# Prompt probabilities transposed in one burst per head pair, selection and prompt values behind the keys, and a later place in the DMA queue for part of the last values

## The chip, the cores and the metric

The kernel runs on one core of a Trainium2 chip. The metric is the device time of one execution in microseconds, taken as the median of several runs. Engines are named as in the profile: PE is TensorE (PEld its weight loads), DVE is VectorE, ACT is ScalarE, POOL is GpSimd, SP is SyncE (SPq its issues of transfers). TensorE has two clock levels, 1.2 and 2.4 GHz; the profile gives the granted clock as a share of the higher one.

## What is computed

One inference step of a two-layer decoder trunk with a width of 2048, for one prompt of 256 tokens and eight decode sequences of eight tokens each, with 2048 past positions in a cache. Each layer is

```python
h = rms_norm(x, g_mix); p = h @ w_in              # columns split among A, B, C
A: dilated sliding-window attention, 8 heads of 64: branches (128,1), (512,4), (2048,16)
B: RWKV-7 time mixing, 8 heads of 64
C: sliding-window attention, window 128, 16 query heads on 2 key heads, with sinks
x = x + concat(A, B, C) @ w_out
x = x + SwiGLU(rms_norm(x, g_ffn))
```

For the prompt, attention is over its own 256 tokens; for a decode token it is over the cached keys and values and the new tokens of its sequence:

```python
s = einsum('bthd,btjhd->bthj', q, k_gathered) * ATTN_SCALE
p = exp(s - logsumexp(s))
o = einsum('bthj,btjhd->bthd', p, v_gathered)
```

The outputs are the new hidden states, the new keys and values, and the new states of B. All data are float32.

## The kernel before

Each engine has its own hand-written instruction stream, and the engines meet at named semaphores: `take("x")` waits for the next count of `x`, `.then_inc` raises it. Nothing reorders the streams, so the order of the lines of an engine is the order in which it works, and an instruction that waits holds back all that stands behind it on its engine. SP issues nearly all transfers, also in the order of its lines.

A layer first streams the projection `w_in` (with B's preparation beside it), then runs B's recurrence, then **attention**, then the projection `w_out` and the SwiGLU weights. The change touches attention alone. The streams of matrix products are bound by TensorE and take most of the time.

Attention has two kinds of work, woven into one another:

- **Prompt work** is twelve pairs of heads, `p` = 0 to 11 (four of A, eight of C). For a pair, TensorE makes the scores (`prompt_scores`, into PSUM banks 0 and 1). VectorE scales, masks and finds the maxima (`front`). ScalarE takes the exponentials (`exp`), VectorE the reciprocal of the sums (`back`), ScalarE multiplies by it (`scale`). TensorE transposes the probabilities, three blocks of 128x128 for each of the two heads, into bank 2; ScalarE copies them to `ppt` (`turned_probs` on both engines). TensorE multiplies them with the values into bank 3 (`prompt_values`), and ScalarE copies the result out (`output`).
- **Sample work** is four passes `q` = 0 to 3, each for two decode sequences. SP loads the cached keys of the two sequences (`cK`, ten tiles of 128x512 each, in three groups per sequence, issued by `next_keys`) and the cached values (`cV`, `next_values`). VectorE transposes the keys in place in 32x32 blocks (`turn`, six groups per pass). TensorE multiplies them with the queries into banks 4 to 7 (`keys`: eight blocks of 32 small matmuls, then the new tokens and the C heads). VectorE scales, masks and finds maxima (`scores`), ScalarE takes exponentials (`exps`), TensorE transposes the probabilities (`probabilities`), ScalarE copies them (`turned_sample`), TensorE multiplies them with the values (`values`). VectorE normalises into `om` (`weighted`); TensorE picks each head's own rows by a matmul with a constant (`select`, into bank 3), and VectorE copies these into `pT` (`outputs`). `window_keys` and `query_rows` prepare the next pass.

In each pass the prompt work of up to three pairs, called `a`, `b` and `carry`, stands between the steps of the sample work. In pass `q` before the change `carry` is pair 3q+2, `a` is 3q+3, `b` is 3q+4 and `c`, whose scores only are made here, is 3q+5; the last pass has `carry` alone. Before the change, the selection of the previous pass, the scores of `a`, the two halves of the transposes of `carry` and the prompt values of `carry` all stand between the eight blocks of `keys`; the transposes and values of `a` and the scores of `b` follow `keys`; those of `b` follow `values`.

For the last pass the values need a place of their own: the early half (sequence 7, `cX`) lies where the outgoing states `Sout` were, so SP waits until these are written (`souts`). Before the change it does so in pass index 1, behind the second keys and ahead of the values of that pass. The other half goes where the first key tile was, once the keys of the last pass are used.

The matmul helper has two lines only: L1492 is every `mm`, L1493 every `tr` (transpose by a matmul with the identity). So in the rows a step is told by its tiles: `PS<-cK,qd` is `keys`, `PS<-con,psm` the transposes of prompt probabilities, `PS<-ppt,tk` the prompt values, `PS<-con,om` the selection, `PS<-con,smA` the sample probabilities, `PS<-cV,ptA` the sample values, `PS<-hh,wh` the output projection behind attention.

Of the kernel before, what the change touches and what calls it, by code (L numbers as in the profile page):

```python
# [37 lines left out]
P = 128  # L38
D = 2048
DEPTH = 2  # L40
SEQ = 256
# [5 lines left out]
HD = 64  # L47
# [127 lines left out]
def build(nc, I, O, at):  # L175
    ctx = ExitStack()
    with ctx:
# [99 lines left out]
        ppt = place("ppt", [P, 2, 384], RW + 44032)  # L277
# [48 lines left out]
        def partners(q):  # L326

            return (3 * q + 3, 3 * q + 4, 3 * q + 5) if q < LASTQ else (None, None, None)
# [34 lines left out]
        def _(sp):  # L363
# [75 lines left out]
            for l in range(DEPTH):  # L439
# [183 lines left out]
        def _(act):  # L623
# [155 lines left out]
            for l in range(DEPTH):  # L779
# [102 lines left out]
                def turned_probs(p):  # L882
                    for h in range(2):
                        take("PT")
                        if p and not h:
                            act.wait_ge(sem["O"], PAIRS * l + p)
                        act.activation(ppt[:, h], PS[:, 2, 0:384], ACT.Copy).then_inc(sem["ptc"], 1)  # L887

                def output(p):
                    take("O")  # L890
                    act.activation(pT[:, tile_of(p), PROMPT], PS[:, 3, 0:SEQ], ACT.Copy).then_inc(sem["oc"], 1)
# [28 lines left out]
                scale(0)  # L920
                turned_probs(0)
                exp(1)
                output(0)
                scale(1)
# [3 lines left out]
                for q in range(NB // 2):  # L928
                    a, b, c = partners(q)
                    carry = 3 * q + 2  # L930
                    exp(carry)
                    scale(carry)
                    turned_probs(carry)
                    if q < LASTQ:
                        exp(a)
                    output(carry)
                    if q < LASTQ:
                        scale(a)
                        turned_probs(a)
                        output(a)  # L940
                    if q == 0:
                        act.wait_ge(sem["snk"], 64 * (l + 1))
                    exps(q)
                    turned_sample(q)
                    if q < LASTQ:
                        query_rows(q + 1)
                        exp(b)
                        scale(b)
                        turned_probs(b)
                        output(b)  # L950
# [5 lines left out]
                split(n0, 0, 0, kts, nd)  # L956
                for g, t0 in enumerate((QA, BR, QC, QC + 4)):
# [20 lines left out]
        def _(dve):  # L978
# [349 lines left out]
            def attention(l):  # L1328
                def front(p):
# [3 lines left out]
                    if p >= 2:  # L1333
                        dve.wait_ge(sem["PT"], 2 * (PAIRS * l + p - 1))
# [50 lines left out]
                def outputs(q):  # L1385
                    take("sel")
                    o = SEQ + 2 * TS * q
                    for hf in range(2):
                        dve.tensor_copy(pT[:, QA + 2 * hf:QA + 2 * hf + 2, o:o + 2 * TS],
                                        PS[:, 3, 256:320].rearrange("p (f h t) -> p h f t", f=2, h=2)[:, hf])  # L1390
                    for b2 in range(2):
                        a = dve.tensor_copy(pT[:, QC:QC + 8, o + b2 * TS:o + b2 * TS + TS],
                                            PS[:, 3, 320 + 64 * b2:384 + 64 * b2].rearrange("p (i t) -> p i t", i=8))
# [5 lines left out]
                turn(0, 1, 2)  # L1399
                back(1)  # L1400
                turn(0, 2, 4)
                front(2)
                turn(0, 4, 6)
                for q in range(NB // 2):
                    a, b, c = partners(q)
                    if q:
                        outputs(q - 1)
                    back(3 * q + 2)
                    if q < LASTQ:
                        front(a)  # L1410
                        back(a)
# [9 lines left out]
                    if q < LASTQ:  # L1421
                        front(c)
# [62 lines left out]
        def _(pe):  # L1485
# [366 lines left out]
            def attention(l):  # L1852
# [30 lines left out]
                def turned_probs(p, h):  # L1883

                    take("pn", 1 - h)
                    if p or h:
                        pe.wait_ge(sem["ptc"], 2 * (PAIRS * l + p) + h)
                    for i in range(3):
# [215 lines left out]
```

## Time and profile before

| | before |
|---|---|
| median of 3 runs | 3384.05 us (3379.69 to 3388.35) |
| the profiled execution | 3381.76 us |
| its span, first to last instruction | 3380.0 us |
| TensorE busy | 3198.1 us, 95% of the span |
| VectorE busy | 1757.8 us, 52% |
| ScalarE busy | 1150.6 us, 34% |
| bytes moved by DMA | 501.29 MB, 148 GB/s over the span |
| granted TensorE clock, mean | 0.962 |

The page of the profile gives busy times over the whole span. The attention stage of the first layer lies at 467 to 648 us, that of the second at 2131 to 2314 us. In the views, a bracket behind a row, such as [7.52 <-DMA cK], is how long the engine stood idle before that instruction and what released it; "issue" means that it waited for nothing that the profile shows. A matmul count is in hardware passes, two for each of these float32 instructions where the row shows the doubled number. The rows of SPq are issues of transfers, not the transfers themselves.

### The profile page before, as it was taken

To read this page: it belongs to the slowest core of one execution; us is meant where nothing else is said; L and a number is where in the kernel's file an instruction comes from. 1 tells how busy PE (TensorE), PEld (TensorE's weight loads), DVE (VectorE), ACT (ScalarE), POOL (GpSimd) and SP (SyncE) were. 2 spreads that over 40 slices of the span, in tenths; PEclk is the share of its full clock that TensorE was granted. 3 is DMA by queue.
4 is the path that set the end of the run, shared out by engine and by line. 5 is a ranking of instruction groups with operands and counts; after the bars stand their busy time and mean duration, and the time that the engine had idled before them with its cause. 6 is when DMAs were issued, how large, how long until landed. Compare 5 with 4: busy or idle time off the path is not lost. (4 is left out here: it accounts for less than half of the span.)

```text
span 3380.0 us, 62858 instructions
## 1 busy us (share of the span) xinstructions
PE 3198.1 (95%) x26358; PEld 3021.7 (89%) x26358; DVE 1757.8 (52%) x2117; ACT 1150.6 (34%) x1543; POOL 74.3 (2%) x157
## 2 busy tenths in 40 slices
PE   8999877799999999999999988778999999999998
PEld 7999744699999999999999986447999999999998
DVE  5455555555555454454545665654555544545544
ACT  3332244433222322322434313543422223223234
POOL 1000010000000000000000000100000000000000
PEclk9999878899999999999999998788999999999999
DMA  6562047665554554654565610677655555545554
GB/s 199 164 135 65 2 155 294 195 151 151 150 149 137 159 149 137 165 149 137 150 187 137 137 27 2 225 286 176 149 149 149 149 140 159 149 139 160 137 148 131
DMA packets 848709, 501.29 MB, mean 148 GB/s; under 512 B 96608, under 2 KB 823152, under 8 KB 848112
## 3 DMA queue, kind: packets, MB, share of 16 engines
q1 hardware_dynamic: 848108, 499.01, 52.6%
q8 instruction: 115, 1.88, 0.2%
q14 instruction: 34, 0.28, 0.0%
q10 hardware_dynamic: 452, 0.11, 0.0%
HBM read 485.71 MB, written 13.37 MB: 148 GB/s over the span
## 5 line engine op out<-in xcount | busy, mean ns | idle before, releaser
L634 ACT ACTIVATE wh<-raw 128x2048 fp32r<-128x2048 f32 (+1 forms) x408 | 711.7, 1744 | 1236.3 <-PE PS L1492 1200.3
L994 DVE TENSOR_TENSOR wl<-raw,wh 128x2048 fp32r<-128x2048 f32 (+1 forms) x408 | 848.8, 2080 | 412.1 <-ACT wh L634 411.4
L1492 PE MATMUL PS<-fh,wh 128*128 128x320 f32 x2816 | 870.6, 309 | 0.0
L1492 PE MATMUL PS<-fl,wh 128*128 128x320 f32 x2816 | 870.1, 309 | 0.0
L1492 PE MATMUL PS<-fh,wl 128*128 128x320 f32 x2816 | 870.1, 309 | 0.0
L1492 PEld LDWEIGHTS PS<-fl,wh 128*128 128x128 f32 x2816 | 528.6, 188 | 0.2
L1492 PEld LDWEIGHTS PS<-fh,wh 128*128 128x128 f32 x2816 | 528.6, 188 | 0.2
L1492 PEld LDWEIGHTS PS<-fh,wl 128*128 128x128 f32 x2816 | 528.6, 188 | 0.0
L1492 PE MATMUL PS<-hh,wh 128*128 128x320 f32 (+2 forms) x1696 | 518.4, 311 | 5.6 <-DVE wl L994 5.6
L1492 PE MATMUL PS<-hh,wl 128*128 128x320 f32 (+2 forms) x1696 | 513.5, 309 | 0.0
L1492 PE MATMUL PS<-hl,wh 128*128 128x320 f32 x1664 | 513.2, 312 | 0.0
L1492 PE MATMUL PS<-ah,wh 128*128 128x320 f32 x1408 | 435.7, 309 | 0.7 <-DVE wl L994 0.5
L1492 PE MATMUL PS<-al,wh 128*128 128x320 f32 x1408 | 435.1, 309 | 0.0
L1492 PE MATMUL PS<-ah,wl 128*128 128x320 f32 x1408 | 435.1, 309 | 0.0
L1492 PEld LDWEIGHTS PS<-hh,wh 128*128 128x128 f32 x1696 | 315.1, 188 | 9.4 <-DVE wl L994 6.1
L1492 PEld LDWEIGHTS PS<-hl,wh 128*128 128x128 f32 x1664 | 314.9, 190 | 1.6 <-DVE hl L1433 0.2
L1492 PEld LDWEIGHTS PS<-hh,wl 128*128 128x128 f32 x1696 | 315.2, 189 | 0.0
L1492 PEld LDWEIGHTS PS<-ah,wh 128*128 128x128 f32 x1408 | 264.3, 188 | 1.4 <-issue 1.2
L1492 PEld LDWEIGHTS PS<-al,wh 128*128 128x128 f32 x1408 | 264.3, 188 | 0.0
L1492 PEld LDWEIGHTS PS<-ah,wl 128*128 128x128 f32 x1408 | 264.3, 188 | 0.0
L663 ACT ACTIVATE ge<-gt 128x320 f32<-128x320 f32 x88 | 41.5, 472 | 488.2 <-DVE gt L1034 488.2
L1034 DVE TENSOR_TENSOR gt<-PS,rsb 128x320 f32<-128x320 f32 x88 | 43.3, 492 | 226.0 <-PE PS L1492 226.0
(327 smaller groups left out, 2554.9 us busy)
## 6 DMA issues: line engine op xcount, KB each, us to landing
raw<-in_w_gate SPq DMA_DIRECT2D x88, 1024.0 KB, 5.6
raw<-in_w_up SPq DMA_DIRECT2D x88, 1024.0 KB, 5.6
raw<-in_w_down SPq DMA_DIRECT2D x128, 704.0 KB, 4.8
raw<-in_w_in SPq DMA_DIRECT2D x56, 1024.0 KB, 5.6
cK<-in_cache_a_k SPq DMA_DIRECT2D x80, 512.0 KB, 9.0
cV<-in_cache_a_v SPq DMA_DIRECT2D x60, 512.0 KB, 10.6
raw<-in_w_in SPq DMA_DIRECT2D x32, 512.0 KB, 5.6
raw<-in_w_out SPq DMA_DIRECT2D x32, 512.0 KB, 4.8
```

What stands on the lines that cost most here:

```text
L634: act.activation(wh[j][:, 0:kts], raw[j][:, 0:kts], ACT.Copy).then_inc(sem["wh"], 1)
L663: act.activation(ge[:], gt[:], ACT.Tanh, scale=0.5).then_inc(sem["gexp"], 1)
L994: tt(wl[j][:, 0:kts], raw[j][:, 0:kts], wh[j][:, 0:kts].bitcast(F32), ALU.subtract).then_inc(sem["wl"], 1)
L1034: tt(gt[:], PS[:, 0, 0:TOK], rsb[:], ALU.mult).then_inc(sem["ev"], 1)
L1492: mm = lambda out, lhsT, rhs, start=True, stop=True: pe.matmul(out, lhsT, rhs, start=start, stop=stop, skip_group_check=True)
```

## The change

Three things are changed, all in attention.

1. The transposes of both heads of a pair are made in one go, six blocks into 768 columns that span bank 2 and the first half of bank 3, and ScalarE copies them with one instruction. The prompt values go into the second half of bank 3, so the transposes of a pair now wait until the previous pair's output has been copied.
2. The pairs are dealt out anew: passes 0 and 1 have `carry`, `a` and `b`, pass 2 has `carry` and `a`, pass 3 has `carry` and `a`. Within `keys` only the scores of `a` (behind the fourth block) and the transposes of `carry` (ahead of the last block) remain. Behind `keys` come the prompt values of `carry`, then transposes and values of `a`, the scores of `b`, and the selection of the previous pass, which now goes into bank 7 and waits for `scores` to have read it (`smb`). The transposes of `b` stand inside `values`, behind its eighth step. On VectorE `front(carry)` to `back(a)` stand ahead of `scores`, `outputs` behind it, and `back(b)` one key group earlier. ScalarE's order follows.
3. SP issues the early half of the last values in pass index 2, behind the third keys, and not in pass index 1. The wait for the written states moves with it.

The core of the diff:

```diff
         def partners(q):
-            return (3 * q + 3, 3 * q + 4, 3 * q + 5) if q < LASTQ else (None, None, None)
+            if q < 2:
+                return 3 * q + 2, 3 * q + 3, 3 * q + 4, 3 * q + 5
+            return (8, 9, None, 10) if q == 2 else (10, 11, None, None)
...
                     if q == 1:
                         states_out()
+                    if q == 2:
                         sp.wait_ge(sem["souts"], 16 * 18 * (l + 1))
                         for quad in range(3):
                             cache(NB - 1, "V", quad)
...
                 def turned_probs(p):
-                    for h in range(2):
-                        take("PT")
-                        if p and not h:
-                            act.wait_ge(sem["O"], PAIRS * l + p)
-                        act.activation(ppt[:, h], PS[:, 2, 0:384], ACT.Copy).then_inc(sem["ptc"], 1)
+                    take("PT")
+                    act.activation(ppt[:], PS[:, 2:4, :].rearrange("p b c -> p (b c)")[:, 0:768], ACT.Copy).then_inc(sem["ptc"], 1)
...
                 for q in range(NB // 2):
-                    a, b, c = partners(q)
-                    carry = 3 * q + 2
+                    carry, a, b, c = partners(q)
                     exp(carry)
                     scale(carry)
+                    exp(a)
                     turned_probs(carry)
-                    if q < LASTQ:
-                        exp(a)
+                    scale(a)
                     output(carry)
-                    if q < LASTQ:
-                        scale(a)
-                        turned_probs(a)
-                        output(a)
+                    turned_probs(a)
                     if q == 0:
                         act.wait_ge(sem["snk"], 64 * (l + 1))
                     exps(q)
+                    output(a)
                     turned_sample(q)
...
-                turn(0, 2, 4)
-                front(2)
-                turn(0, 4, 6)
+                turn(0, 3, 6)
                 for q in range(NB // 2):
-                    a, b, c = partners(q)
+                    carry, a, b, c = partners(q)
+                    front(carry)
+                    back(carry)
+                    front(a)
+                    back(a)
+                    scores(q)
                     if q:
                         outputs(q - 1)
-                    back(3 * q + 2)
                     if q < LASTQ:
-                        front(a)
-                        back(a)
-                    scores(q)
-                    if q < LASTQ:
-                        front(b)
-                        turn(q + 1, 0, 5)
-                        back(b)
-                        turn(q + 1, 5, 6)
+                        if b:
+                            front(b)
+                            turn(q + 1, 0, 4)
+                            back(b)
+                            turn(q + 1, 4, 6)
+                        else:
+                            turn(q + 1, 0, 6)
                     else:
                         split(start_of(l, "out"), 0, KT)
                     weighted(q)
-                    if q < LASTQ:
-                        front(c)
...
-                            if (h, jj) == (0, 0):
-                                if q:
-                                    select(q - 1)
-                                if q < LASTQ:
-                                    prompt_scores(a)
-                            elif (h, jj) == (1, 0):
-                                turned_probs(carry, 0)
-                            elif (h, jj) == (2, 0):
-                                turned_probs(carry, 1)
+                            if (h, jj) == (1, 1):
+                                prompt_scores(a)
                             elif (h, jj) == (3, 0):
-                                prompt_values(carry)
+                                turned_probs(carry)
...
-                        if k == 3 and q < LASTQ:
-                            prompt_scores(partners(q)[2])
+                        if q < LASTQ:
+                            carry, a, b, c = partners(q)
+                            if k == 3:
+                                prompt_scores(c)
+                            elif k == 7 and b:
+                                turned_probs(b)
...
                     keys(q)
-                    if q < LASTQ:
-                        for h in range(2):
-                            turned_probs(a, h)
-                        prompt_values(a)
+                    prompt_values(carry)
+                    turned_probs(a)
+                    prompt_values(a)
+                    if b:
                         prompt_scores(b)
+                    if q:
+                        pe.wait_ge(sem["smb"], 4 * l + q + 1)
+                        select(q - 1)
                     probabilities(q)
                     values(q)
```

## Rows read from the trace of the kernel before

**Rows 1.** Windows, the attention stages: length, busy us per engine, clock, DMA share, GB/s.

```profile
466.90:647.90 181.00, 129.86 (x1961) 77.16 (x1961) 98.51 (x149) 89.25 (x290) 5.73 (x27) 0.80 0.75 266
2130.90:2314.00 183.10, 129.00 (x1965) 76.72 (x1965) 98.28 (x149) 88.90 (x290) 5.25 (x28) 0.82 0.75 263
```

**Rows 2.** Timeline, first layer: start us, length us; first matmul of each pass, then projection.

```profile
490.91 1.38 PE L1492 MATMUL PS<-cK,qd 32*32 32x320 f32 x32 [2.21 <-DVE cK L1354]
...
528.20 0.83 PE L1492 MATMUL PS<-cK,qd 32*32 32x320 f32 x32 [0.47 <-ACT kcT L857]
...
575.24 1.38 PE L1492 MATMUL PS<-cK,qd 32*32 32x320 f32 x32 [0.47 <-ACT kcT L857]
...
614.02 0.83 PE L1492 MATMUL PS<-cK,qd 32*32 32x320 f32 x32 [0.47 <-ACT kcT L857]
...
648.31 2.16 PE L1492 MATMUL PS<-hh,wh 128*128 128x256 f32 x16
```

**Rows 3.** The same of the second layer.

```profile
2154.58 1.38 PE L1492 MATMUL PS<-cK,qd 32*32 32x320 f32 x32 [3.84 <-DVE cK L1354]
...
2191.75 1.38 PE L1492 MATMUL PS<-cK,qd 32*32 32x320 f32 x32 [0.47 <-ACT kcT L857]
...
2240.45 1.38 PE L1492 MATMUL PS<-cK,qd 32*32 32x320 f32 x32 [0.47 <-ACT kcT L857]
...
2279.60 0.83 PE L1492 MATMUL PS<-cK,qd 32*32 32x320 f32 x32 [0.47 <-ACT kcT L857]
...
2313.95 2.16 PE L1492 MATMUL PS<-hh,wh 128*128 128x256 f32 x16
```

**Rows 4.** Timeline, the legs of the first and second pass, first layer.

```profile
512.14 2.57 PE L1493 MATMUL PS<-con,smA 128*128 128x128 f32 x11 [3.38 <-ACT ssk L900]
...
532.72 0.31 PEld L1493 LDWEIGHTS PS<-con,psm 128*128 128x128 f32 x3 [0.74 <-ACT psm L879]
...
542.17 1.69 DVE L1364 SCALAR_TENSOR_TENSOR smA<-PS,con 128x320 f32<-128x320 f32 x4 [3.66 <-PE PS L1492]
...
546.59 1.42 ACT L897 ACTIVATE smA<-smA,snm 128x1344 f32<-128x1344 f32 x1 [1.11 <-DVE snm L1370]
...
549.22 2.13 PE L1493 MATMUL PS<-con,smA 128*128 128x128 f32 x11 [3.31 <-ACT ssk L900]
```

**Rows 5.** Timeline, steps that the change moves: transposes, prompt values, selection.

```profile
524.17 0.55 PE L1493 MATMUL PS<-con,psm 128*128 128x128 f32 x3
...
526.49 0.87 PE L1492 MATMUL PS<-ppt,tk 128*64 128x256 f32 x8 [0.58 <-ACT ppt L887]
...
528.96 0.63 PE L1492 MATMUL PS<-con,om 128*128 128x32 f32 x4
```

**Rows 6.** Timeline, the third keys: the issue ahead of them and the waits behind.

```profile
529.17 1.89 SPq L476 DMA_DIRECT2D cX<-in_cache_a_v  x3
...
556.12 2.31 DVE L1354 STREAM_TRANSPOSE cK<-cK 128x2048 f32<-128x2048 f32 x1 [7.52 <-DMA cK<-in_cache_a_k]
...
565.42 2.31 DVE L1354 STREAM_TRANSPOSE cK<-cK 128x2048 f32<-128x2048 f32 x1 [0.25 <-DMA cK<-in_cache_a_k]
...
569.57 0.90 PE L1493 MATMUL PS<-con,psm 128*128 128x128 f32 x3 [5.47 <-ACT psm L879]
```

**Rows 7.** Windows of 5 us, columns as in the first group.

```profile
555.00:560.00 5.00, 5.00 (x40) 3.18 (x40) 3.72 (x2) 1.98 (x10) 0.00 (x0) 0.50 1.03 402
580.00:585.00 5.00, 5.00 (x132) 2.38 (x131) 1.97 (x3) 1.60 (x5) 0.00 (x0) 0.61 0.01 3
```

**Rows 8.** DMA issues of the whole run: count, KB each, us to landing.

```profile
cK<-in_cache_a_k SPq DMA_DIRECT2D x80, 512.0 KB, 9.0
```

**Rows 9.** Groups by line, whole run: count, busy us, mean ns, idle before.

```profile
L887 ACT ACTIVATE ppt<-PS 128x384 f32<-128x384 f32 x48 | 23.5, 490 | 61.2 <-PE PS L1493 61.2
L907 ACT ACTIVATE ptA<-PS 128x512 f32<-128x512 f32 x16 | 9.5, 597 | 10.5 <-PE PS L1493 10.5
L1354 DVE STREAM_TRANSPOSE cK<-cK 128x2048 f32<-128x2048 f32 x32 | 72.9, 2294 | 21.2 <-DMA cK<-in_cache_a_k 21.0
```

More of the change, by code:

```diff
@@ L276, in build @@
         smC = place("smC", [P, 2, 192], RS + 26880)
-        ppt = place("ppt", [P, 2, 384], RW + 44032)
+        ppt = place("ppt", [P, 768], RW + 44032)
         nm = [place(f"nm{i}", [P, 2, 2], RS + 29184 + 64 * i) for i in range(2)]
@@ L920, in _ @@
                 scale(0)
+                exp(1)
                 turned_probs(0)
-                exp(1)
+                scale(1)
                 output(0)
-                scale(1)
                 turned_probs(1)
@@ L946, in _ @@
                         query_rows(q + 1)
[L947 to L950, printed above, removed]
+                        if b:
+                            exp(b)
+                            scale(b)
+                            turned_probs(b)
+                            output(b)
                         window_keys()
@@ L956, in _ @@
                 split(n0, 0, 0, kts, nd)
+                act.wait_ge(sem["oc"], PAIRS * (l + 1))
                 for g, t0 in enumerate((QA, BR, QC, QC + 4)):
@@ L1881, in prompt_scores, with turned_probs @@
                     a.then_inc(sem["S"], 1)
[L1883 to L1888, printed above, removed]
-                        a = tr(PS[:, 2, i * P:(i + 1) * P], psm[p % 2][:, h, i * P:(i + 1) * P])
+                def turned_probs(p):
+                    take("pn")
+                    if p:
+                        pe.wait_ge(sem["oc"], PAIRS * l + p)
+                    bank = PS[:, 2:4, :].rearrange("p b c -> p (b c)")
+                    for i in range(6):
+                        a = tr(bank[:, i * P:(i + 1) * P], psm[p % 2][:, i // 3, i % 3 * P:(i % 3 + 1) * P])
                     a.then_inc(sem["PT"], 1)
                 def prompt_values(p):
-                    pe.wait_ge(sem["ptc"], 2 * (PAIRS * l + p) + 2)
-                    if p:
-                        pe.wait_ge(sem["oc"], PAIRS * l + p)
-                    if p >= 5 and p % 3 == 2:
-                        pe.wait_ge(sem["bo"], 4 * l + p // 3)
+                    pe.wait_ge(sem["ptc"], PAIRS * l + p + 1)
                     for kt in range(2):
@@ L1902, in prompt_values @@
                             vals = tk[1 if p < 4 else 2][:, kt, c0:c0 + HD]
-                            out = PS[h * HD:h * HD + HD, 3, P * kt:SEQ]
-                            a = mm(out, vals, ppt[:, h, 0:SEQ] if kt == 0 else ppt[:, h, SEQ:384], kt == 0, kt == 1)
+                            out = PS[h * HD:h * HD + HD, 3, SEQ + P * kt:512]
+                            a = mm(out, vals, ppt[:, 384 * h:384 * h + SEQ] if kt == 0 else ppt[:, 384 * h + SEQ:384 * h + 384], kt == 0, kt == 1)
                     a.then_inc(sem["O"], 1)
                 def keys(q):
-                    a, b, c = partners(q)
-                    carry = 3 * q + 2
+                    carry, a, b, c = partners(q)
                     pe.wait_ge(sem["ktc"], 8 * l + 2 * q + 2)
@@ L2008, in attention @@
                 prompt_scores(1)
-                for h in range(2):
-                    turned_probs(0, h)
+                turned_probs(0)
                 prompt_values(0)
                 prompt_scores(2)
-                for h in range(2):
-                    turned_probs(1, h)
+                turned_probs(1)
                 prompt_values(1)
@@ L2017, in attention @@
                 for q in range(NB // 2):
-                    a, b, c = partners(q)
+                    carry, a, b, c = partners(q)
                     keys(q)
-                    if q < LASTQ:
-                        for h in range(2):
-                            turned_probs(a, h)
-                        prompt_values(a)
+                    prompt_values(carry)
+                    turned_probs(a)
+                    prompt_values(a)
+                    if b:
                         prompt_scores(b)
+                    if q:
+                        pe.wait_ge(sem["smb"], 4 * l + q + 1)
+                        select(q - 1)
                     probabilities(q)
@@ L2027, in attention @@
                     if q < LASTQ:
-                        for h in range(2):
-                            turned_probs(b, h)
-                        prompt_values(b)
+                        if b:
+                            prompt_values(b)
                         window_keys(q + 1)
```

18 lines of the change are left out of this document (10 added, 8 removed).

## The prediction

> **What bounds the kernel now.** I read the stretches by stage first. The change lies only in the two attention stages, and there TensorE is busy 129.9 of 181.0 us and 129.0 of 183.1 us, with the DMA engines at 0.75 of their time [rows 1]; everywhere else the kernel is left as it is. No engine is full in these stages, so the order of waits sets their length, and I read that order from the timeline. A stage is a short prologue and four passes, one per pair of decode sequences. In the first layer the key matmuls of the passes begin at 490.91, 528.20, 575.24 and 614.02, and the output projection at 648.31 [rows 2]: passes of 37.3, 47.0, 38.8 and 34.3 us. The second layer has 37.2, 48.7, 39.2 and 34.4 us [rows 3].
>
> A pass has four legs, one behind the other: the **key leg** (matmuls on the old keys, until VectorE can start the scores), the **gap** (mask and maxima on VectorE, exponentials on ScalarE), the **value leg** (transposes of the probabilities, then the matmuls on the old values) and the **tail** to the next key matmul. In the second pass the key leg is 528.20 to 542.17 = 14.0 us and the gap 542.17 to 549.22 = 7.05 us [rows 2, 4]. In the first pass the value leg is 512.14 to 524.17 = 12.0 us and the tail 524.17 to 528.20 = 4.0 us [rows 2, 4, 5].
>
> The second pass is ten microseconds longer than its neighbours, and the reason stands in one place: VectorE sat 7.52 us for the third keys, and TensorE later 5.47 us for the scaled prompt probabilities that VectorE reached only behind the transposes of those keys [rows 6]. The keys were late because SyncE had queued the early half of the last values, at 529.17, ahead of the values of pass 1 and of these keys [rows 6]. The DMA engines moved 402 GB/s at 555 to 560 us and 3 GB/s at 580 to 585 us [rows 7]: a queue in the wrong order, not a lack of bandwidth.
>
> **Part 1, the last values behind the third keys.** Ten issues of 512 KB make one pass's keys (80 issues over eight passes) [rows 8], so 5.4 MB with the small cache; values are the same and the early half of the last values is 2.6 MB. From 529.17 to 565.42, when the fifth of the six key groups had landed [rows 6], the queue moved 2.6 + 5.4 + 4.7 = 12.7 MB: 351 GB/s with the start. After the change only 10.1 MB stand there: 28.8 us. They also start earlier: pass 0 is about 3.5 us shorter up to there (below), and SyncE no longer waits at this point for the states it has written. I put the start at 525.5, so the fifth group lands at 554.3 in place of 565.4. What is moved costs later: the 2.6 MB go in front of the values of pass 2 and the fourth keys. At 402 GB/s the 13.3 MB of those three down to the fifth fourth-key group last 33 us, to 587.4. The values of pass 2 are needed about 582 and land about 575; the fourth keys come just in time (part 3).
>
> **Part 2, work leaves the path.** Selection (528.96 to the next step, 1.0 us) and the prompt values (0.87 us) leave the key leg, and the 0.74 us for which the first half of the transposes waited goes too, because the burst now stands one block from the end [rows 4, 5]. Key leg: 14.0 - 1.0 - 0.9 - 0.7 = 11.4 us. They go into the gap, in which TensorE has about 7 us and gets prompt values (0.9), six transposes, prompt values (0.9), prompt scores (0.9) and selection (1.0), some 5 us with the ScalarE copies between them. Costed at nothing, then; if that cover is gone, the gap grows by what sticks out. Behind the second pair's copy ScalarE has the sample exponentials. By my order that copy ends 3.3 us after the key leg (prompt values 0.9, their copy 0.4, transposes 0.9, copy 0.8, handovers) and the maxima come 4.4 us after it (542.17 to 546.59 [rows 4]), so about 1 us is in hand.
>
> The burst itself: two copies of 128x384 take 0.49 us each, a 128x512 copy 0.60 us [rows 9]. One of 768 is not in the trace: between 0.60 and 0.98; carried on along the two rows it is 0.82. Take 0.82. Now the value matmuls start 2.3 us after the first transpose (524.17 to 526.49) [rows 5]; six transposes, about 0.9 us by two of the 0.55 us rows [rows 5] less their overlap, then 0.82 and two handovers make about 2.0.
>
> In passes 0 and 1 the burst of pair b moves inside the value leg (+1.0 us), so that its copy runs beside the last two value steps. The tail shrinks from 4.0 to about 2.0: values 0.9, window keys, two copies. VectorE's weighting, which the next keys wait for as well, runs beside it and is the shorter. Pass 2 loses pair b altogether (its pair goes into the gap of pass 3), so 3 us of tail go and its value leg keeps its 12.0.
>
> **Part 3, what VectorE and the queues then do.** `outputs` moves behind `scores` and waits for selection, some 2 us later than the scores' maxima; behind it stand `front(b)` and the key transposes, 2.3 us for each of the four large ones [rows 9] and half of it for the two of half the size, 11.5 us together. In pass 1 these transposes start near 545.6 and the fourth ends near 553.8; pair b's scale follows and TensorE waits about 1.2 us for it. The sixth ends near 558, the values near 557.5, the weighting near 559: three ends within 1.5 us. Pass 2: the fourth keys' last transpose ends about 590.7, the weighting, behind the values, about 592. So after the change DMA, VectorE and TensorE are nearly level.
>
> **Sum.** Prologue: TensorE waits 2.21 and 3.84 us for the first keys' transposes [rows 2, 3]; `front(2)` moves behind them, so at most that much: I take 2.0 and 3.0. Pass 0: key leg 13.7 (it starts at the lower clock, its first block 1.38 in place of 0.83 us [rows 2]), gap 7.1, value leg 13.2, tail 2.0: 36.0, a gain of 1.3 and 1.2. Pass 1: 11.4 + 7.1 + 14.2 (with the 1.2 us wait) + 2.1 = 34.8: 12.2 and 13.9. Pass 2: 11.6 + 7.1 + 12.1 + 1.8 = 32.6: 6.2 and 6.6. Pass 3: prompt scores come into its key leg, selection and values go, with the wait about 1.8 each. In the first layer the passes would then begin at 488.9, 524.9, 559.7 and 592.3 and the projection at 624.8. First layer 23.5, second 26.5, together 50 us. Against the profiled execution of 3381.76 us (span 3380.0) that is 3331.8; the median of the three runs, 3384.05, lies 2.3 us higher: 3334.
>
> **Rivals.** *The queue stays the bound.* If the DMA engines hold 350 and not 402 GB/s over the now unbroken 62 us, the third keys end 3 us later and the fourth 8.5 us later than worked out, which nothing hides: 17 us given back, 3351. For it: the 351 GB/s above, and the saturated queue without the pause at 580 us. Against: 402 to 410 once it runs.
>
> *ScalarE late.* If the chain of the second pair is 2.5 us later than I have it, the exponentials start 1.5 us late in each of eight passes: 12 us, 3346. For it: only 1 us is in hand. Against: the chain stands ahead of the exponentials now as well.
>
> *The clock, upward.* The granted clock was 0.50 at 555 to 560 us, the 1.2 GHz level, behind an idle time of TensorE of 3.31 us before the probabilities [rows 4, 7]; the key block takes 1.38 us there and 0.83 us at the 2.4 GHz level [rows 2]. With the gap filled, the longest idle time inside a pass is about 2 us. If all of the passes then run at the higher level, pass 0's key leg gives 1.2 us and pass 3's values about 1.5: 5 us in two layers, 3329. The Trainium skill ("TensorE: Matmul & The Clock Gate", Part 1, "What's actually happening") says that the throttled state is the default and activity releases it, which speaks for this rival. The trace agrees [rows 4, 7]; by that rule alone the time would be 3329.
>
> *The clock, downward: slower than before.* The new idle times are shorter but more numerous. If they hold TensorE at the lower level through the passes, a key leg of eight blocks alone costs 8 x 0.55 = 4.4 us more, in proportion 7 for the whole leg, 4 for the value leg and 2 for the rest: 13 us a pass, 104 in all, 3438. From about half of that on the gain is gone. Against it: now the low level follows the long idle times, and these go.
>
> *It doesn't do what it says:* the gap work sticks out by as much as it saves and only the queue's order acts. Then passes 1 alone give, some 9 us each: 3366.
>
> **How the numbers follow.** Forecast 0.55, the queue 0.16, ScalarE 0.08, clock upward 0.10, only the queue's order 0.04, clock half downward (no change) 0.03, wholly downward 0.04. Range 3316 to 3356: it takes the forecast with its bounds (copy 0.60 to 0.98 us on twelve bursts a layer, prologue, a bubble of 1 us in each key leg), both middle rivals and the upward clock, and leaves 0.11 out above plus some tail below. About 0.3% (10 us) is what a measurement of this kernel can tell from no change. Faster 0.93, within it 0.03, slower 0.04.
>
> **What would show it.** Right: the second pass no longer than its neighbours, about 35 us; no VectorE wait of 7 us on keys; one 768-column copy per pair near 0.82 us; selection and prompt values between the key leg and the probabilities, with the gap still near 7.1 us; key legs near 11.4. Wrong, if VectorE waits for fourth keys, if the exponentials start more than 0.2 us behind the maxima, or if the granted clock of the stages falls below the 0.80 and 0.82 of now [rows 1].

## The result, and the profile after

| | before | after |
|---|---|---|
| median | 3381.87 us (3378.37 to 3388.35, 4 runs) | 3341.43 us (3331.34 to 3343.31, 4 runs) |
| ratio, 95% interval | | 0.9873 [0.9858, 0.9888] |
| profiled execution, its span | 3381.76, 3380.0 us | 3341.29, 3339.5 us |
| mean granted clock | 0.962 | 0.968 |

The change saves 40.5 us by the spans. 3334 was predicted, 7 us too low, inside the range of 3316 to 3356. Windows over the attention stages of the kernel after (columns as in [rows 1]):

```profile
465.40:627.40 162.00, 121.82 (x1964) 76.63 (x1965) 98.30 (x149) 86.29 (x278) 6.55 (x32) 0.84 0.84 298
2110.00:2272.60 162.60, 120.67 (x1964) 76.77 (x1965) 98.42 (x149) 86.40 (x278) 5.86 (x28) 0.86 0.84 296
```

Against [rows 1] the stages are 19.0 and 20.5 us shorter, all but one microsecond of the gain. Timeline of TensorE, first layer: the first key matmuls of the passes and the output projection, which answer to [rows 2].

```profile
487.08 1.38 PE L1490 MATMUL PS<-cK,qd 32*32 32x320 f32 x32 [0.47 <-ACT kcT L860]
...
520.46 0.83 PE L1490 MATMUL PS<-cK,qd 32*32 32x320 f32 x32 [0.47 <-ACT kcT L860]
...
560.83 1.59 PE L1490 MATMUL PS<-cK,qd 32*32 32x320 f32 x58 [0.47 <-ACT kcT L860]
...
595.30 0.96 PE L1490 MATMUL PS<-cK,qd 32*32 32x320 f32 x33 [0.92 <-DVE omC L1381]
...
627.42 2.16 PE L1490 MATMUL PS<-hh,wh 128*128 128x256 f32 x16
```

The second layer has its passes at 2129.45, 2161.65, 2202.63 and 2240.46 and the projection at 2272.61. Gains by pass, from these times and [rows 2, 3]:

| gain, us, first / second layer | predicted | measured | pass is now |
|---|---|---|---|
| prologue | 2.0 / 3.0 | 2.3 / 4.2 | 21.7 / 19.5 |
| pass 0 | 1.3 / 1.2 | 3.9 / 5.0 | 33.4 / 32.2 |
| pass 1 | 12.2 / 13.9 | 6.7 / 7.7 | 40.4 / 41.0 |
| pass 2 | 6.2 / 6.6 | 4.3 / 1.3 | 34.5 / 37.8 |
| pass 3 | 1.8 / 1.8 | 2.2 / 2.2 | 32.1 / 32.2 |
| stage | 23.5 / 26.5 | 19.4 / 20.4 | |

Three steps of the second pass came out close to the forecast or better. The start of the scores on VectorE, of the exponentials on ScalarE and of the transposes of the probabilities, which answer to [rows 4]:

```profile
530.45 1.68 DVE L1363 SCALAR_TENSOR_TENSOR smA<-PS,con 128x320 f32<-128x320 f32 x4 [0.92 <-PE PS L1490]
...
534.88 1.42 ACT L897 ACTIVATE smA<-smA,snm 128x1344 f32<-128x1344 f32 x1 [1.45 <-DVE snm L1369]
...
537.50 1.42 PE L1491 MATMUL PS<-con,smA 128*128 128x128 f32 x11 [1.26 <-ACT ssk L900]
```

Key leg 520.46 to 530.45 = 10.0 us, gap 7.05 us as before, and the exponentials still wait for the maxima, not for the copy of the burst. That copy, in the groups by line (count, busy us, mean ns, idle before):

```profile
L887 ACT ACTIVATE ppt<-PS 128x768 f32<-128x768 f32 x24 | 19.3, 803 | 19.2 <-PE PS L1491 19.2
```

0.80 us, where 0.82 was taken. What fell short stands in pass 1, at the third keys, as in [rows 6]:

```profile
544.39 2.31 DVE L1353 STREAM_TRANSPOSE cK<-cK 128x2048 f32<-128x2048 f32 x1 [5.45 <-DMA cK<-in_cache_a_k]
...
550.96 2.31 DVE L1353 STREAM_TRANSPOSE cK<-cK 128x2048 f32<-128x2048 f32 x1 [0.59 <-DMA cK<-in_cache_a_k]
...
553.60 3.44 DVE L1353 STREAM_TRANSPOSE cK<-cK 128x2048 f32<-128x2048 f32 x2
...
555.11 1.54 PE L1491 MATMUL PS<-con,psm 128*128 128x128 f32 x6 [7.73 <-ACT psm L882]
```

and in the value leg of pass 2:

```profile
579.16 1.54 PE L1491 MATMUL PS<-con,smA 128*128 128x128 f32 x11 [2.12 <-ACT ssk L900]
...
586.61 3.64 PE L1490 MATMUL PS<-cV,ptA 128*32 128x256 f32 x32
```

In pass 1 VectorE still waits 5.45 us for keys and TensorE 7.73 us, more than the 5.47 us of before, for pair b's scaled probabilities behind four transposes. In pass 2 the 32 value matmuls take 3.64 us, at the lower clock; in pass 0 they take 1.93.

### The profile page after: what moved, and what is told of

It reads as the page before. It is cut to its first block, busy times and chain, and to the rows that moved or that the text cites. A ratio compares the mean times of both kernels' runs of the same rounds, so it can differ in the third digit from the quotient of the medians.

```text
span 3339.5 us, 62764 instructions
## 1 busy us (share of the span) xinstructions
PE 3181.0 (95%) x26358; PEld 3019.1 (90%) x26358; DVE 1757.0 (53%) x2117; ACT 1145.1 (34%) x1519; POOL 73.8 (2%) x157
## 4 chain that ended last, share of the span: by engine, by line
PE 89%; DVE 4%; SPq 2%; DMA 2%; ACT 1%; issue 1%; ACTq 0%; DVEq 0%
PE PS L1490 87%; PE PS L1491 2%; DMA cK<-in_cache_a_k 1%; SPq L510 1%; SPq L478 1%; DVE wl L993 0%; DMA raw<-in_w_down 0%; SPq L480 0%; ACT wh L637 0%; DVE S0T L1286 0%; DMA sink<-in_c_sink 0%; DVE smA L1363 0%; DVE rt L1111 0%; DVE snm L1368 0%; DMA raw<-in_w_in 0%
```

## Experiments

**The two halves by themselves.** x1_queue_only is the kernel before with the last values moved in the queue and nothing else; x2_queue_undone is the changed kernel with that one step taken back.

```diff
# x1_queue_only, against before; x2_queue_undone takes this line out of the changed kernel
                     if q == 1:
                         states_out()
+                    if q == 2:
                         sp.wait_ge(sem["souts"], 16 * 18 * (l + 1))
```

> The kernel before with one part of the change alone: the early half of the last values is issued behind the third keys. Theory (the place in the queue of transfers is a gain of its own): the third keys land about 9 us earlier, VectorE's wait for them falls from 7.5 us to under 2, the second pass falls from 47.0 and 48.7 us to about 38 and 39, the others stay within 1 us: about 3364 us. Rival (the moved 2.6 MB only make the fourth keys late): the second pass gains and the third loses as much, 3380 us.

> The changed kernel with that one part undone: the early half of the last values stands again ahead of the values of the second pass. Theory: in the second pass the third keys end it, so it grows by the transfer time of the 2.6 MB and its issues, 7 to 8 us per layer, from 40.4 to about 48: 3356 us. Rival (VectorE's order ends that pass, not the queue): under 2 us per layer, 3344. Other rival (nearly all of the gain is the queue's): close to the kernel before, above 3370.

Measured: x1 3375.1 us, 0.998 [0.9968, 0.9993]; x2 3357.0 us, 0.9909 [0.9891, 0.9927]. So, by the medians, the queue's order is worth 8.7 us without the other edits and 15.6 us on top of them; the other edits are worth the rest, 25 to 32 us. The intervals (2 to 11 us for the first) do not tell the two apart. In x2 the passes 1 are 45.3 and 48.0 us, and VectorE waits 9.71 and 13.67 us for the third keys; the first of these waits:

```profile
555.00 2.31 DVE L1352 STREAM_TRANSPOSE cK<-cK 128x2048 f32<-128x2048 f32 x1 [9.71 <-DMA cK<-in_cache_a_k]
```

In x1 VectorE's waits for the third keys are gone and passes 1 are 37.4 and 41.1 us in place of 47.0 and 48.7, but passes 0 are 41.0 and 41.8 in place of 37.3 and 37.2. Passes 2 are 2.3 and 1.4 us longer too, but VectorE doesn't wait for the fourth keys, so it is not as the rival had it. The value legs of passes 0 and 2 run at a granted clock of 0.50 in both layers of x1, where before they had 0.82 to 1.00. The windows of 515 to 520 us, in the value leg of pass 0, first of x1, then of before:

```profile
515.00:520.00 5.00, 4.26 (x50) 2.57 (x48) 4.66 (x3) 3.44 (x20) 0.00 (x0) 0.50 1.03 391
```

```profile
515.00:520.00 5.00, 4.27 (x75) 2.59 (x77) 5.00 (x4) 3.83 (x22) 0.00 (x0) 0.94 1.06 380
```

TensorE is equally busy but at half the clock, so it gets through 50 and not 75 matmuls. The edit does not touch this leg, and the clock there differs between executions of one kernel (the changed kernel's second trace, below, shows it). In these traces that hides part of what the queue gives. That a moved transfer pays more where the work that waits for it is quicker would fit the two medians, but is not shown.

**Is it the placement?** x8_key_leg is the changed kernel with selection and prompt values back between the key blocks.

```diff
+                            if (h, jj) == (0, 0):
+                                if q:
+                                    select(q - 1)
...
+                    prompt_values(carry)
                     take("qbd")
...
                     keys(q)
-                    prompt_values(carry)
...
-                    if q:
-                        pe.wait_ge(sem["smb"], 4 * l + q + 1)
-                        select(q - 1)
```

> The changed kernel with selection and the carried pair's prompt values back in the key leg (the burst and the queue order stay). Theory (these steps were on the path, the gap hid them): key legs of 10.0 become 11 in pass 0 and 12 in passes 1 to 3, the gap stays 7.05. In pass 1 the wait for the third keys takes it in, in the other three it counts: 0.9 + 1.9 + 1.9 = 4.7 us a layer, 3351. Rival 1: the emptier gap also brings the lower clock back into the value legs, 2 to 3 us a layer more: 3356. Rival 2: off the path, within 2 us of 3341.

Measured: 3351.0 us (3339.1 to 3356.3), 0.9894 [0.9871, 0.9917]; 9.6 us over the first median of the changed kernel, as the theory had it, though the two intervals overlap. Its places were only half right. Pass 3 grew by 2.6 and 2.9 us, its key leg from 10.0 to 13.1: selection, prompt values and a wait of 1.21 us for the copy of the burst. Pass 1 took its share in, as expected. But the largest growth, 4.1 and 5.2 us, is in pass 0, of which the key leg has at most 1.0: its emptier gap left TensorE idle for 3.92 and 3.93 us, and the value leg then ran at the lower clock, which is rival 1. So the key leg of pass 3 shows that the gap hid the moved work. That the filled gap also keeps the clock in pass 0 is likely, not shown by this run alone. From the start of the transposes of the probabilities the granted clock over 9.3 us is 0.53 and 0.50 here. Behind 2.36 or 2.37 us of idle time it is 1.00 in 9 of the 11 passes 0 of that kind and 0.56 and 0.57 in the other two, one of them in the changed kernel itself; in the kernel before, behind 3.38 us, it is 0.82 and 1.00.

**The lower clock in pass 2.** x6_fill puts 14, 6, 14 and 14 transposes of the identity at the end of the four gaps; nothing reads them.

```diff
                         select(q - 1)
+                    for _ in range((14, 6, 14, 14)[q]):
+                        tr(PS[:, 2, 0:P], C("ident"))
                     probabilities(q)
```

> The changed kernel with 14, 6, 14 and 14 transposes of a constant by TensorE, whose results nobody reads, at the end of the gap of the four passes. Theory (the value leg of the third pass is 14.8 instead of 12.1 us because TensorE runs it at the lower clock level behind an idle time of 2.1 us): the granted clock in that leg goes from 0.5 to 1.0 and the leg to about 12.2; with the fourth pass some 2 to 4 us per layer, 3335 us. Rival (the level in that leg does not hang on the idle time just ahead of it): the leg stays at 14 to 15 us, and the probabilities start up to 0.5 us later, 3341 to 3344.

Measured: 3335.1 us, 0.9853 [0.9837, 0.987], an interval that overlaps that of the changed kernel. In the second layer the value leg of pass 2 runs at the higher clock:

```profile
2224.91 1.70 PE L1491 MATMUL PS<-con 128*128 128x128 f32 x14
2226.93 1.42 PE L1491 MATMUL PS<-con,smA 128*128 128x128 f32 x11 [0.32 <-ACT ssk L900]
...
2232.14 1.93 PE L1490 MATMUL PS<-cV,ptA 128*32 128x256 f32 x32
```

From the probabilities to the next keys it is 12.0 us in place of 17.3 (first layer 12.8 in place of 16.1). The other traces bear this out. With the filler (x6, twice x7, x14) the granted clock over the 9.3 us from the probabilities is 1.00 in all 30 passes in which the filler left 0.3 to 0.7 us of idle time; in the twelve passes 2 of the changed order without it, behind 1.4 to 2.5 us, it is 0.50 to 0.85. So filling the idle time ahead of the probabilities keeps the clock of this leg. The time of the pass is another matter: in the first layer pass 2 took 37.6 us, 3.1 more than without the filler, because its key leg was 14.3 us and its gap 10.6: TensorE had fallen to the lower clock in the key leg already, and there the filler alone takes 3.19 us and no longer fits. Why it fell is the next experiment's subject.

**The idle time with nothing to wait for.** In x4_states_last SyncE issues the states and the early last values behind the fourth keys.

```diff
                     next_keys(q)
-                    if q == 1:
+                    if q == LASTQ:
                         states_out()
-                    if q == 2:
                         sp.wait_ge(sem["souts"], 16 * 18 * (l + 1))
```

> The changed kernel with SyncE's 18 issues of the written states, and the early half of the last values that waits for them, put behind the fourth keys. Theory (the queue still ends the second pass, because the values ahead of the third keys are issued behind the 17 us of those 18 issues): the values start some 8 us earlier, VectorE's wait of 5.45 us for the third keys goes, the second pass falls from 40.4 and 41.0 to about 33 to 35 us; the third may become the one that the queue ends, up to 37: 3327 to 3333 us. Rival (TensorE is held by the scale of pair b, which stands behind four key transposes on VectorE whatever the keys do): the second pass stays above 39, 3340.

Measured: 3342.3 us, 0.9864 [0.9845, 0.9884]: nothing gained, though no wait for third keys is left. The key legs of pass 1 are 14.7 and 15.5 us in place of 10.0 and 10.1. TensorE in the first of them, in x4:

```profile
526.60 2.43 PE L1489 MATMUL PS<-cK,qd 32*32 32x320 f32 x95
530.80 0.42 PE L1489 MATMUL PS<-cK,qd 32*32 32x320 f32 x1 [1.76 <-issue]
...
532.26 1.37 PE L1489 MATMUL PS<-cK,qd 32*32 32x320 f32 x32
```

It stops one matmul short of a block's end for 1.76 us, with no semaphore behind the wait ("issue"), and the next block runs at the lower clock (1.37 us). In the changed kernel SyncE is busy with the 18 issues of the states from 506.1 to 523.1 us, and the transfers run at 89 GB/s in the same place; in x4 they run at 326 and 405. Windows of the changed kernel and of x4 (520 to 525 and 525 to 530 us):

```profile
520.00:525.00 5.00, 4.54 (x169) 2.83 (x170) 2.53 (x6) 2.86 (x13) 0.00 (x0) 1.00 0.43 89
```

```profile
520.00:525.00 5.00, 4.53 (x135) 2.76 (x140) 3.83 (x9) 2.33 (x6) 0.00 (x0) 1.00 1.01 326
525.00:530.00 5.00, 4.03 (x138) 2.13 (x129) 2.31 (x5) 3.94 (x17) 0.00 (x0) 1.00 1.03 405
```

That suggested that TensorE runs short of instructions while the transfers are saturated. x10_quiet tests it the other way: in the changed kernel it holds SyncE back until the key leg of pass 2 is through.

```diff
                     if q == 2:
+                        sp.wait_ge(sem["sc"], 4 * l + q + 1)
                         sp.wait_ge(sem["souts"], 16 * 18 * (l + 1))
```

> The changed kernel, but SyncE issues nothing more for the last values and the values of pass 2 until the key leg of pass 2 is through, so that the DMA engines are quiet in that leg. It is meant to be slower: the fourth keys land some 10 us later in each layer, about 3361. What it is for is the key leg of pass 2, now 11.3 and 13.5 us with TensorE idle for 0.58 and 1.86 us with nothing to wait for (issue). Theory (under saturated transfers TensorE runs out of instructions): with the transfers quiet this idle time is gone and the leg is 10.0 to 10.3 us in both layers, as in pass 3. Rival (it belongs to the place in the program or to chance): 0.6 to 1.9 us of it stay, and the leg stays over 11.

Measured: 3370.8 us, 0.9965 [0.9955, 0.9976], VectorE waiting 19.8 and 19.5 us for the fourth keys. The key leg of pass 2 is 10.0 and 10.3 us with no such idle time. Second layer, first the changed kernel, then x10:

```profile
2206.60 0.79 PE L1490 MATMUL PS<-cK,qd 32*32 32x320 f32 x22
2209.24 2.26 PE L1490 MATMUL PS<-cK,qd 32*32 32x320 f32 x74 [1.86 <-issue]
2211.44 0.87 PE L1491 MATMUL PS<-con,psm 128*128 128x128 f32 x6
```

```profile
2221.29 2.45 PE L1491 MATMUL PS<-cK,qd 32*32 32x320 f32 x96
2223.67 0.88 PE L1492 MATMUL PS<-con,psm 128*128 128x128 f32 x6
```

All 104 key legs of the thirteen traces say the same. Where the transfers of a leg's first 8 us ran at 10 GB/s or less, none of 26 has an "issue" idle time of 0.4 us or more; at 360 GB/s or more 47 of 53 have one, 1.1 us a leg in the mean of all 53, up to 3.2; in between 7 of 25. The list of DMA queues has one that carries instructions (queue, kind: packets, MB, share):

```profile
q8 instruction: 115, 1.88, 0.3%
```

These are 16 KB a packet. The Trainium skill ("Runtime: NRT & Kernel Launch", "Instruction fetch mechanics") says that an engine's instructions come in blocks of 16 KiB, 256 instructions, over a DMA queue of their own while it executes, and that crossing a block boundary is mostly hidden. The packets agree in size; the hiding holds here with quiet transfers and fails with saturated ones.

The traces tie the idle times to these packets. All 58 "issue" idle times of 0.4 us or more in the key legs end 1.25 to 1.61 us behind the end of the last such packet before them. The one of x4 above ends at 530.80, and this is the packet before it, from the view of x4's DMA queues at 528.3 to 528.5 us:

```profile
q8 instruction: 1, 0.02, 27.9%
```

27.9% of 16 engines' 0.2 us is 0.89 us, so the packet, begun within this window, had landed near 529.3, and TensorE went on 1.5 us later. In the six traces that share the order of TensorE's work the idle times stand at nine places of it, the same ones in every trace, and within a layer these lie 127 to 128 matmuls with as many weight loads apart (some 255 instructions) or a multiple of that. At the place where the changed kernel stood for 1.86 us, x10 ran on: there the packet had landed 2.3 us before TensorE came to the place. So TensorE waits here for its own instructions, which come late while the transfers are saturated. What holds the packets back is not shown: that of x10 took 0.94 us, no less than that of x4, so it is their start that is late.

**The order behind the late keys.** x5_scale_first moves two steps of VectorE in pass 1; x7_both has the filler of x6 as well.

```diff
                             front(b)
+                            if q == 1:
+                                back(b)
                             turn(q + 1, 0, 4)
-                            back(b)
+                            if q == 1:
+                                weighted(q)
+                            else:
+                                back(b)
                             turn(q + 1, 4, 6)
...
-                    weighted(q)
+                    if q != 1:
+                        weighted(q)
```

> The changed kernel with two steps of VectorE moved in the second pass alone: the sums of pair b (`back(b)`) stand ahead of the transposes of the third keys, not behind four of them, and `weighted` stands ahead of the last two. Theory (the third keys' landing is amplified by the order behind it): TensorE's idle time of 7.7 and 8.2 us before the burst of pair b goes below 3, `weighted` runs while VectorE has transposes left, and the next keys start as soon as the sixth transpose is done, 557.0 in place of 560.8 in the first layer: passes of 40.4 and 41.0 us become 37.5 to 38, about 3335. Rival 1: the fourth keys come no earlier, so pass 2 grows by what pass 1 gives: 3341. Rival 2: only the idle time moves (TensorE waits the same at the next keys): pass 1 stays above 40.

> The moved VectorE steps of x5 together with the filler transposes of x6 (14, 6, 14 and 14 transposes of the identity at the end of the gap, whose result nothing reads). Theory: the two gains are in different passes (pass 1, and the value leg of passes 2 and 3 at the full clock) and add up: 3335 of x6 less 5 to 6, so 3329 to 3331. Rival: the fourth keys' landing fixes the end of pass 2, so that what pass 1 gives is taken back there: 3335.

Measured: x5 3335.4 us (3325.9 to 3343.6), 0.9868 [0.9849, 0.9887]; x7 3331.7, 0.9845 [0.9829, 0.9861]. Both intervals overlap that of the changed kernel, so what x5 does is read from its passes. Passes 1 of x5 are 38.2 and 37.9 us (theory 37.5 to 38) and pass 2 doesn't give it back (33.8 and 33.1). TensorE and VectorE of x5 at the end of pass 1:

```profile
546.07 0.88 PE L1497 MATMUL PS<-con,psm 128*128 128x128 f32 x6
...
557.45 3.08 PE L1496 MATMUL PS<-cK,qd 32*32 32x320 f32 x66 [2.60 <-issue]
```

```profile
553.91 3.44 DVE L1353 STREAM_TRANSPOSE cK<-cK 128x2048 f32<-128x2048 f32 x2
557.27 0.92 DVE L1335 SCALAR_TENSOR_TENSOR psm<-PS,con 128x768 f32<-128x768 f32 x1
```

The burst of pair b no longer waits, and the keys start 0.2 us behind the last transpose: the pass is now set by the keys' landing and six transposes alone. ("issue" here most likely covers a wait for VectorE that had just been met: unlike in the 58 idle times above, the last instruction packet had landed 6.4 us before.)

**The changed kernel and x7 side by side, and the states moved once more.** In x14_states_third, on top of x7, the states go behind the third keys.

```diff
-                    if q == 1:
-                        states_out()
                     if q == 2:
+                        states_out()
```

> The changed kernel once more, on the same chip as the next two: 3341 by the first measurement, with single runs between 3331 and 3344 as the granted clock of the run has it.

> The kernel of x7 once more, beside the changed kernel: 3332, and 8 to 10 us under it, if both of its gains are real; within 4 us of it, if 3331.7 was the luck of a run with a high clock.

> x7, with the 18 issues of the states moved from ahead of the values of pass 1 to behind the third keys, so that the transfers don't pause in the key leg of pass 1 and the third keys land earlier. Theory (the pause was the cover of that key leg): VectorE's wait for third keys of 5 us goes, but the key leg of pass 1 gets an idle time of 1 to 2 us with nothing to wait for, falls to the lower clock behind it and takes 13 to 15 us in place of 10.0; pass 1 lies within 2 us of x7's 39.2 and 38.5, the whole within 4 us of x7. Rival 1: the landing counts for more than the pause: passes 1 of 35 us, 3324. Rival 2: the states, issued later, hold up the last values and the fourth keys: pass 2 grows by 3 us or more in each layer, 3340.

Measured: the changed kernel 3337.5 us (3337.1 to 3347.4), 0.9876 [0.9858, 0.9893]; x7 3330.3 (3328.5 to 3332.0), 0.9847 [0.9833, 0.9861]; x14 3350.6, 0.9909 [0.9893, 0.9924]. The ranges of the first two don't touch: x7 is 7 us faster, the fastest kernel here. Its two parts were not measured finely enough to say what each gives.

x14 lost 20 us to x7, and rival 2 was right: VectorE waits 5.33 and 7.11 us for the fourth keys. The theory was right on the key legs of pass 1, 13.8 and 14.3 us with 1.64 and 2.41 us of "issue". What it had not seen is that with keys in time the order of x5 does harm:

```profile
549.24 0.16 DVE L1342 TENSOR_TENSOR sums<-sums,psk 128x4 f32<-128x4 f32 x1 [5.08 <-ACT psk L873]
549.43 0.18 DVE L1343 RECIPROCAL sums<-sums 128x4 f32<-128x4 f32 x1
549.87 7.83 DVE L1352 STREAM_TRANSPOSE cK<-cK 128x2048 f32<-128x2048 f32 x4 [0.26 <-DVE sums L1343]
```

VectorE waits 5.08 us for pair b's exponentials while the keys lie ready. That order pays only where the keys come later than these.

The second trace of the changed kernel is the best witness on pass 1. Its pass 0 ran at the lower clock and took 37.4 us, not 33.4; its pass 1 took 34.1, not 40.4:

```profile
548.47 7.83 DVE L1353 STREAM_TRANSPOSE cK<-cK 128x2048 f32<-128x2048 f32 x4
...
558.13 0.87 PE L1491 MATMUL PS<-con,psm 128*128 128x128 f32 x6 [1.26 <-ACT psm L882]
```

No wait for keys, 1.26 us for pair b, and a stage of 162.3 us against 162.1: what pass 0 lost, pass 1 gave back here.

## Why the prediction was right, and where it was off

**What bounds the kernel: right.** The order in SyncE's queue and TensorE's steps on the path were the two levers, worth 9 to 16 us and 25 to 32 us by the medians (x1, x2). The sum of the gains was 10 us too high: 8.7 us too little in some legs and 18.9 us too much in others. That the total came this near is in part luck.

**Too little: prologue, pass 0, pass 3** (8.7 us over both layers), and a key leg of 11.4 us that is 10.0. Of these 1.4 us, 0.97 is an "issue" idle time in the leg of before, ahead of the prompt values, which the sum took for work:

```profile
537.80 0.79 PE L1492 MATMUL PS<-cK,qd 32*32 32x320 f32 x21 [0.97 <-issue]
538.52 0.87 PE L1492 MATMUL PS<-ppt,tk 128*64 128x256 f32 x8
```

Pass 0 gained 2.6 and 3.8 us more than worked out. Of this 0.8 and 2.6 us are in the key leg (12.94 and 11.11 us, 13.7 was taken); in the second layer this leg now runs at a granted clock of 1.00, where it had 0.79. The other 1.9 and 1.2 us are behind the gap, in the first layer by the clock of the value leg: 1.42 us for the first eleven transposes where [rows 4] have 2.57. In the second layer these took 1.42 us before as well. This is the upward rival, true in part for passes 0 and 1 and not for 2 and 3; so the stages have a clock of 0.84 and 0.86, not 0.80 and 0.82 and not 1.

**Too much: pass 1** (11.7 us). The landing was right: the fourth transpose was forecast to end near 553.8 and ended near 553.2, and the next keys at 559.7 came at 560.83. What failed is the wait of 1.2 us for pair b's scale. It was worked out with TensorE arriving late; it arrived 7 us earlier than that at the same landing (4.4 by the start of the pass, 1.4 by the key leg, the rest by the clock of the value leg), waited 7.73 us, and then ran the last steps at the lower clock (1.54 us for six transposes, 0.88 in pass 0). Where pass 0 was slow (the second trace) the wait was 1.26 us and the pass 34.1, against 1.2 and 34.8 forecast. The prediction's closing remark, three engines level within 1.5 us, named the point but priced it as if all terms were exact: every microsecond won ahead of a fixed landing is worth nothing.

**Too much: pass 2** (7.2 us). Two terms were missing. Its value leg was taken at 12.0 us, the higher clock; it ran at the lower one, at 2.12 and 2.47 us of idle time (x6: with 0.32 us the leg runs at the higher one). And its key leg, now under saturated transfers, has "issue" idle times of 0.58 and 2.46 us, of which a bubble of 1 us stood only in the range. x4 and x10 show that these come and go with the transfers.

**The rivals.** *Queue stays the bound*: not as it was put; the queue ran at 398 to 412 GB/s from 535 to 585 us, and no fourth key was waited for by over 0.6 us, though the third keys' landing still ends pass 1. Its price was too high in itself: the sum already takes the third keys at 351 GB/s, so 350 in place of 402 would delay only the 13.3 MB behind them, by 4.9 us a layer and not 8.5, which makes 3344 and not 3351. *ScalarE late*: no; even in x4's second pass of the second layer, with the gap work at the lower clock, the exponentials start 4.4 us behind the key leg. But TensorE's own work in the gap sticks out there, with no idle time ahead of the probabilities, and the gap is 9.19 us:

```profile
2180.81 1.55 PE L1489 MATMUL PS<-ppt,tk 128*64 128x256 f32 x8 [0.90 <-ACT ppt L886]
2182.28 1.65 PE L1489 MATMUL PS<-pT 64*128 64x128 f32 x8
2183.87 1.06 PE L1489 MATMUL PS<-con,om 128*128 128x32 f32 x4
2184.74 1.09 PE L1489 MATMUL PS<-con,omC 128*128 128x64 f32 x4
2185.63 2.56 PE L1490 MATMUL PS<-con,smA 128*128 128x128 f32 x11
```

The cover that the second part was costed at nothing for is 2 us short at the lower clock. *Clock downward* and *only the queue's order*: no.

**What would show it.** Gap, copy, placement and VectorE's maxima were as listed; "the second pass no longer than its neighbours" was not, and it was the sign that pass 1 still hung on the keys.

## What to carry to other kernels

Where a landing fixes the end of a stretch, compare it with the arrival of the work after all other gains are in, and put nothing that a third engine needs behind the transposes that wait for it, unless the landing comes early (x14). A burst of transfers that fills the queue can also make TensorE's instructions late, as it did here, so look at the "issue" idle times of the longest instruction streams before filling a pause in the queue. Filling a wait with work that is off the path pays twice where it keeps TensorE's clock (x6), and its cost must be checked at the lower clock as well.

## What the runs showed of the hardware

- TensorE stands idle for up to 2.4 us at a time, with no semaphore behind it, in the key legs (286 small matmuls in 10 us) while the transfers run at 360 GB/s or more, and in none of 26 legs with quiet transfers. Of all key legs' idle times of this kind, 58 are of 0.4 us or more, and each ends 1.25 to 1.61 us behind the landing of a 16 KB instruction packet.
- One such idle time of 1.4 to 1.8 us was followed by the 1.2 GHz level in x4 and x6 (a block of 32 key matmuls took 1.30 to 1.37 us, not 0.82); behind those of 1.44 and 1.51 us in the passes 0 of x6 the granted clock of the key leg stayed at 1.00.
- The same program had its pass 0 at the higher clock in one execution and partly at the lower in the next (33.4 and 37.4 us), with 2.37 and 2.36 us of idle time ahead of the probabilities: in the first the clock stayed up behind it, in the second it fell. The length of one idle time doesn't settle the clock.
